# A hybrid decoder step on one core: exponentials ahead of filler copies, split state steps, later sample scores

## The reference, cut to what matters

```python
b = jnp.cumsum(lfc, axis=2)
diff = jnp.where(causal[None, None, :, :, None],
                 b[:, :, :, None, :] - b[:, :, None, :, :], -jnp.inf)
att = jnp.einsum('bhtk,bhsk,bhtsk->bhts', qc, kc, jnp.exp(diff))
o = jnp.einsum('bhts,bhsv->bhtv', att, vc) + jnp.einsum('bhtk,bhkv->bhtv', qc * jnp.exp(b), S)
S_new = jnp.exp(b_last[:, :, 0, :])[..., None] * S + jnp.einsum(
    'bhsk,bhsv->bhkv', kc * jnp.exp(b_last - b), vc)
```

```python
z = jnp.einsum('bqhd,bkhd->bhqk', q, k) * (HD_A ** -0.5) + bias[None, :, None, None]
log_keep = jnp.where(mask, jax.nn.log_sigmoid(-z), 0.0)
later = lax.cumsum(log_keep, axis=3, reverse=True) - log_keep
w = jnp.where(mask, jnp.exp(jax.nn.log_sigmoid(z) + later), 0.0)
```

## Time and profile before

| what | us |
|---|---|
| median of 3 runs | 1934.62 |
| lowest and highest | 1932.97, 1934.95 |
| the profiled execution's own time | 1933.75 |
| its span | 1932.1 |
| busy: TensorE matmuls | 1865.4 |
| busy: VectorE | 999.9 |
| busy: ScalarE | 568.4 |
| busy: GpSimd | 422.3 |

### The profile page before, as it was taken

The page is one execution under the profiler, slowest core; times in us unless marked ns, Lnnn a source line. Parts: engine busy times, 40 slices in busy tenths (PEclk is TensorE's granted clock), DMA queues, the critical chain, the costliest instruction groups (busy, mean ns, idle before and its releaser), DMA issues.

```text
span 1932.1 us, 28618 instructions
## 1 busy us (share of the span) xinstructions
PE 1865.4 (97%) x11857; PEld 1796.9 (93%) x11857; DVE 999.9 (52%) x1170; ACT 568.4 (29%) x764; POOL 422.3 (22%) x213
## 2 busy tenths in 40 slices
PE   8999999899899999999999999999999999999998
PEld 5999888797678999999899999999999999999998
DVE  6922374643576122121434766866766766685522
ACT  4133423215464122121334321221221231133610
POOL 2322312122112122221211210221121121022221
PEclk9999999899999999999999999999999999999999
DMA  5311212114414222222311110110110111011121
GB/s 197 37 66 67 67 53 82 49 68 175 120 50 151 78 89 70 76 77 100 111 67 66 66 44 22 65 43 22 65 54 27 49 54 43 33 66 37 49 78 45
DMA packets 54294, 134.26 MB, mean 69 GB/s; under 512 B 12834, under 2 KB 28738, under 8 KB 51906
## 3 DMA queue, kind: packets, MB, share of 16 engines
q1 hardware_dynamic: 42114, 105.40, 15.9%
q0 software_dynamic: 5184, 19.01, 3.0%
q10 hardware_dynamic: 6912, 8.65, 1.3%
HBM read 110.82 MB, written 22.31 MB: 69 GB/s over the span
## 4 chain that ended last, share of the span: by engine, by line
PE 91%; DVE 3%; issue 2%; ACT 2%; DMA 1%; SPq 1%; POOL 0%; ACTq 0%; POOLq 0%; DVEq 0%
PE ps L703 60%; PE ps L1120 10%; PE ps L685 8%; PE pst L1120 3%; PE ps L848 2%; PE ps L666 2%; PE ps L769 1%; PE ps L672 1%; PE ps L927 1%; PE pst L948 1%; PE ps L961 1%; DVE Ml L2015 0%; SPq L521 0%; DMA masks<-in_wb 0%; SPq L522 0%
## 5 line engine op out<-in xcount | busy, mean ns | idle before, releaser
L2247 POOL TENSOR_TENSOR Ul<-BIG,Uh 128x1024 fp32r<-128x1024 f32 x60 | 145.2, 2421 | 709.7 <-ACT Uh L1559 630.3
L703 PE MATMUL ps<-Nh,Uh 128*128 128x352 f32 x1248 | 271.0, 325 | 3.9 <-issue 2.2
L703 PE MATMUL ps<-Fl,Uh 128*128 128x352 f32 x1248 | 269.5, 324 | 0.0
L703 PE MATMUL ps<-Nh,Ul 128*128 128x352 f32 x1248 | 269.5, 323 | 0.0
L703 PEld LDWEIGHTS ps<-Nh,Uh 128*128 128x128 f32 x1248 | 213.0, 189 | 5.1 <-issue 4.9
L703 PEld LDWEIGHTS ps<-Nh,Ul 128*128 128x128 f32 x1248 | 214.9, 188 | 0.0
L703 PE MATMUL ps<-Hh,Uh 128*128 128x352 f32 x936 | 203.7, 326 | 9.6 <-DVE Ml L2015 4.3
L703 PEld LDWEIGHTS ps<-Fl,Uh 128*128 128x128 f32 x1248 | 212.5, 188 | 0.0
L703 PE MATMUL ps<-Hh,Ul 128*128 128x352 f32 x936 | 202.4, 324 | 0.0
L703 PEld LDWEIGHTS ps<-Hh,Uh 128*128 128x128 f32 x936 | 159.4, 189 | 12.4 <-issue 5.0
L703 PEld LDWEIGHTS ps<-Hh,Ul 128*128 128x128 f32 x936 | 161.4, 189 | 0.0
(11 more groups left out here) (318 smaller groups left out, 3196.5 us busy)
## 6 DMA issues: line engine op xcount, KB each, us to landing
BIG<-in_wu SPq DMA_DIRECT2D x44, 512.0 KB, 3.6
H<-in_wd SPq DMA_DIRECT2D x11, 1024.0 KB, 4.8
BIG<-in_wgl SPq DMA_DIRECT2D x20, 512.0 KB, 4.3
BIG<-in_x SPq DMA_DIRECT2D x16, 528.0 KB, 6.0
gates<-BIG ACTq DMA_DIRECT2D x48, 176.0 KB, 1.9
BIG<-in_wz POOLq DMA_DIRECT2D x16, 512.0 KB, 3.8
BIG<-gates SPq DMA_DIRECT2D x12, 528.0 KB, 3.7
BIG<-in_wge POOLq DMA_DIRECT2D x12, 512.0 KB, 3.8
```

The source lines that it names most:

```text
L703: ins = nc.tensor.matmul(psb(3 * out + g), w[wp][:, k], x[xp][k][:, t0:t0 + n], start=(k == 0 and wp == xp), stop=(k == kk - 1 and wp == 1))
L2247: nc.gpsimd.tensor_tensor(Ul[:, half], uraw[:, half], Uh[:, half].bitcast(F32), ALU.subtract)\
```

## The change: what it does

In the recurrence ScalarE makes the exponentials of level 0 before it copies out the two `states` fillers; the exponentials of level 1 come behind these copies. VectorE does the first three of the eight state steps, then factors 0, differences 1, the other five state steps, select 0 and factors 1. From level 2 on the order is as it was.

In the attention the second group of sample scores moves from step 10 to step 12, and the filler of step 12 to step 10. The new keys' scores follow pair 6 (step 15) in place of pair 4 (step 11). VectorE's add of group 1 moves from item 11 to item 13, and ScalarE's copy of the new keys' scores from item 12 to item 16.

```diff
-SCORES_AT = (4, 10)
-NEW_AFTER = 4
+SCORES_AT = (4, 12)
+NEW_AFTER = 6
...
-FILL_STEPS = {s: j for j, s in enumerate((0, 2, 6, 8, 12, 14, 16, 18, 20, 22, 24, 28, 30))}
+FILL_STEPS = {s: j for j, s in enumerate((0, 2, 6, 8, 10, 14, 16, 18, 20, 22, 24, 28, 30))}
...
-                for p in parts(f"states{i}"):
-                    gate_out(p)
-                for l, m in enumerate(LEVELS):
+
+                def exponents(l, m):
                     n = len(LEVELS) * i + l
...
                     nc.scalar.activation(ev[:, :, 1, :], dv[:, :, 1, :], ACT.Exp).then_inc(S("b_exps"), 1)
-                    if l:
-                        gate_out(parts(f"levels{i}")[l - 1])
+                exponents(0, LEVELS[0])
+                for p in parts(f"states{i}"):
+                    gate_out(p)
+                for l, m in enumerate(LEVELS[1:]):
+                    exponents(l + 1, m)
+                    gate_out(parts(f"levels{i}")[l])
...
-                def prompt_states():
+                def prompt_states(cs):
                     dve.wait_ge(S("b_ufree"), 2 * i + 1)
-                    link(v.tensor_copy(Sall[:, 0, :], UBp[:, 0, :]))
-                    for c in range(1, NCH):
+                    for c in cs:
                         link(v.scalar_tensor_tensor(Sall[:, c, :], Sall[:, c - 1, :], bdec[:, c:c + 1], UBp[:, c, :],
-                                                    ALU.mult, ALU.add))
+                                                    ALU.mult, ALU.add) if c else v.tensor_copy(Sall[:, 0, :], UBp[:, 0, :]))
...
-                for l in range(NL + 1):
+                differences(0, LEVELS[0])
+                prompt_states(range(3))
+                factors(0, LEVELS[0])
+                differences(1, LEVELS[1])
+                prompt_states(range(3, NCH))
+                select(0)
+                factors(1, LEVELS[1])
+                for l in range(2, NL + 1):
                     if l < NL - 1:
                         differences(l, LEVELS[l])
-                    if l >= 1:
-                        select(l - 1)
-                    else:
-                        prompt_states()
+                    select(l - 1)
                     if l < NL - 1:
                         factors(l, LEVELS[l])
```

## The result

| kernel | median us | lowest, highest | runs |
|---|---|---|---|
| before | 1934.21 | 1932.97, 1934.95 | 4 |
| after | 1921.44 | 1917.37, 1923.07 | 4 |

The ratio is 0.9932 with the 95% interval 0.992 to 0.9944: 12.8 us faster, where 14.7 were forecast (1919.9).

A forecast was written before the change was run, and what follows sets the result against it. TensorE, busy 97% of the span, was taken as the bound, so only its stands could be regained: 5.3 (block 0) + 3.6 (block 1) + 5.8 (attention) = 14.7 us, giving a median of 1919.9, range 1916.2 to 1924.6.

The forecast's parts named there:

- Block 0: First level of the recurrence: earlier factors remove TensorE's 3.70 us stand and the 1.59 of low clock behind it, 5.3 us.
- the copies of the fillers: Recurrence: ScalarE's later filler copies are cheap; the first waits until 242.4, its bank is not refilled before 247.6.
- Block 1, the port: Block 1 factors: GpSimd's weight split blocks VectorE on the SBUF port, about 1.7 us of TensorE stand comes back.
- the second product: Block 1 factors: ahead of GpSimd's subtraction, or behind it with TensorE standing 0.4 to 0.5 us at level 0.
- Block 1, the time: First level of block 1: 5.3 less 1.7 of returning stand gives 3.6 us gained, 5.3 if nothing is blocked.
- Rival (b): Block 1's level-1 stand is long enough to drop the clock: 12.9 us gained, 1921.7; chance 0.14.
- no fall: Block 1, level 1: a 1.7 us stand is taken to leave the clock up; a fall would cost 1.5 to 2 us.
- The attention: Sample scores' group 1 at step 12 avoids the page wait: step-14 filler 6.4 us earlier, 5.8 net.
- the new keys: Attention: the four moved new-key matmuls come back at step 15 and cost 0.56 us of the 6.4.
- Downstream: After the attention: everything is released by TensorE's own counts, so it moves along and the gain is kept.
- (d): Rival: the next stage is paced by a transfer that does not follow TensorE, much given back, 1931 to 1935; chance 0.05.
- (e): Rival: VectorE becomes the pacer of the recurrence levels, late at each of 14 factor waits, slower at 1939; chance 0.03.

The follow-up runs named there:

- e4: ScalarE's exponentials first, but all eight VectorE state steps ahead of the first factors, old attention; 1931.13 us, ratio 0.998 against before.
- e7: VectorE's state steps split, ScalarE's exponentials in the old late order, old attention; 1934.69 us, ratio 1.0004 against before.
- e9: Changed kernel plus 40 matmuls with unread results ahead of TensorE's 7.4 us wait in block 1; 1916.13 us, ratio 0.9908 against before.
- e10: e6 plus 40 matmuls with unread results ahead of TensorE's 7.4 us wait in block 1; 1914.85 us, ratio 0.9902 against before.
- e1: The changed kernel run and profiled again, no edit; 1921.59 us, ratio 0.9935 against before.
- e2: Changed kernel with the old attention steps, so the recurrence half alone; 1929.06 us, ratio 0.9972 against before.
- e12: Changed kernel with the old order of ScalarE and VectorE in block 0 only; 1924.29 us, ratio 0.9951 against before.
- e3: Kernel before with only the attention half of the change, old recurrence; 1928.32 us, ratio 0.9967 against before.
- e5: Changed kernel with GpSimd's second weight split in block 1 waiting until behind the factors; 1922.09 us, ratio 0.9933 against before.
- e6: e5 plus VectorE's add of the score groups ahead of its copy of heads; 1921.96 us, ratio 0.9933 against before.
- e8: Changed kernel with group 0 of the sample scores moved from step 4 to 6, filler to step 4; 1928.41 us, ratio 0.997 against before.
- e11: Kernel before plus 40 matmuls with unread results ahead of TensorE's 7.4 us wait in block 1; 1930.43 us, ratio 0.9984 against before.

## Why the prediction was right, and what its sum had wrong

**Block 0: right.** 5.4 against 5.3, at the places named: factors before TensorE wants them, level-0 matmuls in 1.99, no stand at level 1. e4 and e7 show that the order of the exponentials does it alone. That the copies of the fillers cost nothing when later held too: nothing in the waits points at them.

**Block 1, the port: right.** The prediction left open whether the second product goes ahead of the subtraction or behind it. In the profile after it went behind: 2.87 us, and then 1.9 us of stand, where 1.7 were forecast. They came as 1.06 at level 0, where 0.4 to 0.5 were forecast, and 0.87 at level 1. e9 and e10 show the cause. The Trainium skill, SBUF — State Buffer, section "Who interferes with whom", on which the prediction drew there, agrees with 0.69 (e10) against 2.87 (e9) for the same product. But the prediction took it that TensorE's fillers keep their place. Where the low clock delays them (e1, e2), the split comes after the factors, and no stand of 1 to 2 us is there.

**Block 1, the time: mis-sized.** The term was 3.6; it measured 3.0 in the profile of the fastest run and 1.3 in e1. With the old block 0 and its short low stretch it was 3.2 (e12). The sum took over the matmuls at line 826 to the fillers as they stood in the trace of before, 3.71, 1.91 and 7.85. They hang on a stand of 7.43 us that the change does not touch, at a moment that it does touch. In the changed kernel the clock stayed low twice as long behind it in most profiles: 4.0 us, which removed the 1.9 of stands. The 2.0 net are about what is missing, 14.7 - 12.8. By e1's profile the sum is less neat: block 1 is 2.3 under its term, the first stretch and the way to group 0 are together 0.95 over before, and 0.7 come back elsewhere. Rival (b) gave 1921.7, close to the median, and it was still the wrong mechanism: it had the new stands lower the clock, and behind stands of 1.06 and 0.87 the matmuls took 2.06, against 1.99 elsewhere, at a clock of 1.00. Nor does the length of a stand alone decide, as (b) and the choice of "no fall" had it. The stand of 2.21 at line 672, behind which the earlier trace rows has 0.66, left the clock at 1.00 in the profile after (its 12 matmuls took 3.79, not 5.48), and the clock fell there only behind stands of 0.97 and 1.05.

**Which kernels have the long stretch.** By the profiles, short: before, e3, e7, e12, and the changed kernel's first profile; long: e1, e2, e4, e5, e6, e8. All with ScalarE's old order in block 0 are short, and all with the new one are long but for one execution. Within a kernel, the time follows the mean granted clock of the run: of the four runs of the first comparison, the five of e1 and the five of e5, those at 0.989 took 1921.7 to 1923.4, those at 0.991 1921.0 to 1921.6, and those at 0.992 to 0.994 1917.4 to 1920.6. The mean doesn't tell at which place the clock was low. e9 and e10 show that without the stand the loss is gone. e9 gains 5.5 us over the change (1921.59 to 1916.13), of which the profiles of e1 and e9 have 4.6 between level 1 of block 0 and level 1 of block 1. e11 gains 3.9 over before, with a wide scatter (1926.55 to 1935.67).

Why it is long in the one and short in the other is not settled. Block 0's order, over 80 us earlier, changes two things: the moment of the stand moves by 5.4 us, and the clock's past is another one, since block 0's own low stretch is gone. No run separated the two. The profiles lean to the moment: the stand ends at 342.2 to 344.4 from the start of the span in the four of the old order, at 336.7 to 338.6 in the six long ones, and at 334.4 in the changed kernel's first profile, which has the new order's past and is short all the same. The low clock at block 0's updates doesn't decide it: of the long ones, e2 and e8 are without it. With one profile of each run, this is a pattern and not a cause shown.

**The attention: right.** 6.4 to the filler as forecast, with 0.6 of wait on the add where 0.5 was forecast; the new keys came back at 0.56. By the next filler the gain is 5.7 net, where 5.8 was forecast; e3 measured 6.1 alone. e6 and e8 confirm the two mechanisms, the queue of VectorE and the 16 issues on SP's queue.

**Downstream: right to within the scatter.** From the step-14 filler to the end are 1420.31 before, and 1420.41 and 1420.3 in the two profiles of the changed kernel. Over all 14 profiles this stretch goes from 1417.6 to 1421.9, in e3 it is 1.6 longer than before, so it can't confirm a term of half a microsecond. Nothing the size of (d) or (e) happened. Ahead of the attention the change does give back 0.8 in one profile and 0.2 in the other (the second stand at line 672), which the prediction put at nothing.

## What to carry to other kernels

A time read from a trace in a stretch behind a long stand of TensorE is not a constant: here the matmuls behind one took 4 us more in most profiles with an edit over 80 us earlier, so put its bound into the range, and look whether the stand itself can be filled. When an order is moved earlier, look at what other engines do at the new moment, not only at what the engine waited for. When a wait disappears from a second profile, compare the matmul durations in front of it before calling it solved.

## What the runs showed of the hardware that was not expected

- Behind the same stand of 7.43 us in the same program, the granted clock was low for about 7 us in one execution and about 15 in another, which is 3.7 us more for the same matmuls (line 830 at 3.71 and not 2.27, the two fillers at 10.08 and not 7.80). The Trainium skill, TensorE: Matmul & The Clock Gate, gives the two levels that the rows show. The difference between executions was not expected.
- 40 matmuls without a use, placed in that stand, shorten the whole by 5.5 us in the changed kernel and 3.9 in the one before.
- A lower clock of TensorE can take away a clash between two other engines: in e1 it delayed the filler that starts GpSimd's cast, and VectorE's products took 0.69 and not 1.08 and 2.87.
- GpSimd is held too: the subtraction beside VectorE's factors took 2.71 in e4, and 2.39 beside one state step before; the mean of the 60 of line 2253 is 2.42 on the page after.
- Issuing a page load costs the SP queue about 1.1 us, 16 of them 17.85 us (e8), and this, not the transfer of about 2.0 us, set how far apart the two groups must stand.
